# A new order of projection tiles, pooling products inside the attention steps, and an output projection that begins on the pooling groups

## The reference, cut to what matters

```
h = rmsnorm(x);  p, q, k, v = split(h @ w_in)              # 4 x 512 columns
d_g = windowed_mean(p_g, w_g) - p_g                        # 4 pooling groups of 128 columns, w = 2, 4, 8, 16
pool_g = (d_g @ pool_w_g) * pool_scale_g
q, k = rope(q), rope(k)
per head h (4 heads, two score maps each), query block i of 128 rows, keys 0 .. (i+1)*128:
    attn = softmax(q1 k1) - lam * softmax(q2 k2);  o = attn @ v
o = rmsnorm_per_head(o);  x = x + concat(pool_0..3, o_0..3) @ w_o
```

## Time and profile before

| | us |
|---|---|
| three runs | 1964.58, 1962.74, 1958.37 |
| median | 1962.74 |
| the profiled execution's own time | 1960.72 |
| its span, first to last instruction | 1958.6 |
| mean granted TensorE clock | 0.972 |
| first attention step to the end of `wo` | about 50 to 238.6 |

### The profile page before, as it was taken

One profiled execution on the slowest core, in us unless ns is written; L12 is line 12 of the kernel. 1 busy time (PEld: TensorE's weight loads), 2 busy tenths in 40 slices (PEclk: granted clock), 3 DMA queues, 4 the chain that ended last, 5 costly groups with the idle time before them and its releaser, 6 DMA issues.

```text
span 1958.6 us, 23662 instructions
## 1 busy us (share of the span) xinstructions
PE 1836.3 (94%) x8380; PEld 1486.7 (76%) x8380; DVE 1140.8 (58%) x1721; ACT 657.1 (34%) x978; POOL 204.5 (10%) x150
## 2 busy tenths in 40 slices
PE   6996999999999999999999998888898999999986
PEld 4675888888888888888776776667776888888864
DVE  6466668888334655532343777788666655552256
ACT  4333422333223222222333334444444322232242
POOL 3221000000000000000023334444000000000000
PEclk9997999999999999999899999999999999999998
DMA  4676222223322232333222333221241323332221
GB/s 141 71 75 49 86 97 96 96 96 104 102 91 79 97 96 96 100 103 104 80 76 76 105 123 118 69 88 43 93 153 56 108 96 96 96 119 101 90 67 54
DMA packets 55460, 180.62 MB, mean 92 GB/s; under 512 B 6336, under 2 KB 7104, under 8 KB 55392
## 3 DMA queue, kind: packets, MB, share of 16 engines
q1 hardware_dynamic: 43200, 157.07, 24.3%
q10 hardware_dynamic: 12192, 22.67, 7.2%
HBM read 167.65 MB, written 12.06 MB: 92 GB/s over the span
## 4 chain that ended last, share of the span: by engine, by line
PE 77%; DVE 14%; ACT 3%; issue 3%; DMA 2%; ACTq 0%; DVEq 0%; SPq 0%; POOL 0%
PE bank L743 20%; PE bank L744 20%; PE bank L745 20%; PE bank L765 2%; PE bank L767 2%; PE bank L766 2%; PE bank L839 2%; PE bank L840 1%; PE bank L841 1%; DVE score L2206 1%; DMA raw<-in_w_proj 1%; DVE best L2205 1%; PE bank L814 1%; PE bank L1132 1%; DVE chunk L1872 1%
## 5 line engine op out<-in xcount | busy, mean ns | idle before, releaser
L1197 ACT ACTIVATE w_hi<-raw 128x1024 fp32r<-128x1024 f32 (+2 forms) x281 | 304.6, 1087 | 743.7 <-PE bank L745 640.8
L743 PE MATMUL bank<-a_hi,w_hi 128*128 128x512 f32 x1272 | 500.6, 394 | 14.6 <-DVE w_lo L1775 4.9
L745 PE MATMUL bank<-a_hi,w_lo 128*128 128x512 f32 x1272 | 496.6, 390 | 0.0
L744 PE MATMUL bank<-a_lo,w_hi 128*128 128x512 f32 x1272 | 496.6, 390 | 0.0
L1775 DVE TENSOR_TENSOR w_lo<-raw,w_hi 128x1024 fp32r<-128x1024 f32 (+2 forms) x219 | 280.4, 1281 | 253.8 <-ACT w_hi L1197 241.2
L743 PEld LDWEIGHTS bank<-a_hi,w_hi 128*128 128x128 f32 x1272 | 239.7, 188 | 76.8 <-issue 18.9
L745 PEld LDWEIGHTS bank<-a_hi,w_lo 128*128 128x128 f32 x1272 | 239.6, 188 | 50.7
L744 PEld LDWEIGHTS bank<-a_lo,w_hi 128*128 128x128 f32 x1272 | 240.0, 189 | 48.8
L655 POOL TENSOR_TENSOR w_lo<-raw,w_hi 128x1024 fp32r<-128x1024 f32 x54 | 130.0, 2408 | 1071.3 <-ACT w_hi L1197 1071.3
L743 PE MATMUL bank<-h_hi,w_hi 128*128 128x512 f32 x568 | 221.0, 389 | 0.0
L744 PE MATMUL bank<-h_lo,w_hi 128*128 128x512 f32 x568 | 221.0, 389 | 0.0
(11 more groups left out here) (297 smaller groups left out, 2210.6 us busy)
## 6 DMA issues: line engine op xcount, KB each, us to landing
raw<-in_w_up SPq DMA_DIRECT2D x132, 512.0 KB, 3.4
raw<-in_w_down SPq DMA_DIRECT2D x48, 704.0 KB, 4.1
raw<-in_w_proj SPq DMA_DIRECT2D x59, 512.0 KB, 3.5
raw<-in_w_wo SPq DMA_DIRECT2D x8, 512.0 KB, 4.8
raw<-in_w_branch SPq DMA_DIRECT2D x16, 256.0 KB, 2.8
gates_in<-spill ACTq DMA_DIRECT2D x16, 256.0 KB, 3.2
raw<-in_w_out SPq DMA_DIRECT2D x8, 512.0 KB, 3.9
raw<-in_w_ple SPq DMA_DIRECT2D x8, 512.0 KB, 3.4
```

The source lines that it names most:

```text
L743: mm(dst[:, :], wh, hi[:, k, :], start=(first and c == 0), stop=False)
L744: mm(dst[:, :], wh, lo[:, k, :], start=False, stop=False)
L745: step = mm(dst[:, :], wl, hi[:, k, :], start=False, stop=(last and c == n - 1))
L1197: fn(w_hi[:, slot, 0:size], raw[:, slot, 0:size], ACT.Copy).then_inc(unit_high, 1)
```

## The change

The order of the projection tiles becomes q0 k0 v0 q1 k1 p3 v1 q2 k2 p2 v2 q3 k3 p1 v3 p0, the host lays out `w_proj1` in this order, and the steps take 8, 7, 7, 8, 7, 7, 8, 8, 8, 8, 8, 6, 6, 8, 0, 0 chunks, so that the last projection tile ends in step 13. The product of pooling group 3, 2, 1, 0 is done in step 5, 9, 13, 15 respectively; DVE scales it in that step, ACT makes its high part in that step, DVE its low part in the next. The output projection takes the chunks in the order pool 3, 2, 1, 0, heads 0 to 3: tiles 0 to 2 take pool 3 in step 14, pool 2 in step 15, pool 1 in step 16, pool 0 after step 17. Tile 3 takes its four pooling chunks after head 3's sums and ahead of the four `spread` products; then tiles 0 and 1 take the heads' chunks as they come, then tiles 2 and 3. For `mix_hi` of a pooling group to lie over a used q, the q of head h is stored in slot 3-h; `pool_d` shrinks to two buffers and the softmax buffers move up by four tiles.

```diff
-TILES1 = [(kind, h) for h in range(HEADS) for kind in "qkv"] + [("p", g) for g in range(len(WINDOWS))]
+TILES1 = [("q", 0), ("k", 0), ("v", 0), ("q", 1), ("k", 1), ("p", 3), ("v", 1), ("q", 2), ("k", 2), ("p", 2),
+          ("v", 2), ("q", 3), ("k", 3), ("p", 1), ("v", 3), ("p", 0)]
+POOL_ORDER = (3, 2, 1, 0)
+POOL_AT = {5: 3, 9: 2, 13: 1, 15: 0}
+MIX_ORDER = POOL_ORDER + (4, 5, 6, 7)
-FILL1 = spread(LEAD1, len(TILES1), [7] * ATT_STEPS)
+FILL1 = spread(LEAD1, len(TILES1), [8, 7, 7, 8, 7, 7, 8, 8, 8, 8, 8, 6, 6, 8, 0, 0])
-for _g in range(len(WINDOWS)):
-    _aux("pool", _g)
+    if _a in POOL_AT:
+        _aux("pool", POOL_AT[_a])
+        r1.at[0] += len(WINDOWS) * T * 4
# PE
+            def out_part(i, at):
+                first, k = UNIT["wo"][0], MIX_ORDER[at]
+                if at == 0:
+                    wait_bank("wo", i)
+                    pe.wait_ge(unit_split, first + i + 1)
...
+                mm(dst[:, :], wh, mix_hi[:, k, :], start=(at == 0), stop=False)
+                mm(dst[:, :], wh, mix_lo[:, k, :], start=False, stop=False)
+                step = mm(dst[:, :], wl, mix_hi[:, k, :], start=False, stop=(at == DC - 1))
+                if at == DC - 1:
+                    step.then_inc(unit_done, 1)
+            def out_chunk(at, tiles):
+                pe.wait_ge(act_ready, SPLIT["mix1"] + at + 1)
+                for i in tiles:
+                    out_part(i, at)
...
+                if ATT_STEPS - 2 <= a <= ATT_STEPS:            # after fill and aux1
+                    out_chunk(a - ATT_STEPS + 2, range(3))
...
+                if a in POOL_AT:                               # after the turn of a-1
+                    g = POOL_AT[a]
+                    dst = aux_wait("pool", g)
+                    pe.wait_ge(pool_ready, POOL_ORDER.index(g) + 1)
+                    mm(dst[:, :], pool_w[:, g, :], pool_d[:, g % 2, :], start=True, stop=True).then_inc(aux_ready, 1)
...
-                if a == ATT_STEPS:
-                    for g in range(len(WINDOWS)):
-                        dst = aux_wait("pool", g)
-                        pe.wait_ge(pool_ready, g + 1)
-                        mm(dst[:, :], pool_w[:, g, :], pool_d[:, g, :], start=True, stop=True).then_inc(aux_ready, 1)
-            first_three("wo", "mix1", mix_hi, mix_lo, spread_after=(1, 2, 2, 3))
-            for i in range(3, DC):
-                project("wo", i, None, mix_hi, mix_lo)
+            out_chunk(3, range(3))
+            sum_head("head", HEADS - 1)
+            for at in range(HEADS):
+                out_part(3, at)
+            aux_all_free(AUX_ATT)
+            for h in range(HEADS):
+                spread(f"head{h}")
+            for at in range(HEADS, DC):
+                out_chunk(at, range(2))
+            for i in (2, 3):
+                for at in range(HEADS, DC):
+                    out_part(i, at)
+            for i in range(4, DC):
+                project("wo", i, None, mix_hi, mix_lo)
# ACT, end of a step
+                if a in POOL_AT:
+                    g = POOL_AT[a]
+                    high(SPLIT["mix1"] + POOL_ORDER.index(g), mix_hi[:, g, :])
+                if a == ATT_STEPS - 1:
+                    load_root_table()
                 if a == ATT_STEPS:
-                    load_root_table()
-                    highs("mix1", 0, 4, mix_hi)
-            unit_high_part(UNIT["wo"][0] + 3)
+                    unit_high_part(UNIT["wo"][0] + 3)
# DVE
+            def scale_pool(g):
+                c = SPLIT["mix1"] + POOL_ORDER.index(g)
+                dve.wait_ge(aux_ready, AUX["pool", g] + 1)
+                slot_free(c)
+                step(v.tensor_scalar(chunk[:, c % 2, :], aux_bank("pool", g)[:, :], prm("pool_scale", g), None,
+                                     ALU.mult))
+                dve.sem_inc(aux_sem("pool", g), 1)
+                dve.sem_inc(chunk_ready, 1)
...
+                if a - 1 in POOL_AT:                           # after attn of a-1
+                    g = POOL_AT[a - 1]
+                    low(SPLIT["mix1"] + POOL_ORDER.index(g), mix_lo[:, g, :], mix_hi[:, g, :])
...
+                if a in POOL_AT:                               # after rotate, ahead of pool_difference
+                    scale_pool(POOL_AT[a])
...
-            for g in range(4):
-                c = SPLIT["mix1"] + g
-                dve.wait_ge(aux_ready, AUX["pool", g] + 1)
...
-                low(c, mix_lo[:, g, :], mix_hi[:, g, :])
```

More of the change, by code:

```diff
@@ L205 @@
         _aux("bias", _a)
-for _g in range(len(WINDOWS)):
-    _aux("pool", _g)
+    if _a in POOL_AT:
+        _aux("pool", POOL_AT[_a])
+AUX_ATT = len(AUX)
 IDX_STEPS = [(i, h) for i in (3, 2, 1) for h in range(DSA_HEADS)]
@@ L406, in two_blocks @@
         pool_s = r1("pool_s", [P, 2, PAD + T])
-        pool_d = r1("pool_d", [P, 4, T])
+        pool_d = r1("pool_d", [P, 2, T])
         mix_hi = placer(q1_at, q1_at + DC * T * 4)("mix_hi", [P, DC, T], F32R)
@@ L824, in total_x, with first_three @@
                 spread(name)
-            def first_three(stage, split, hi=a_hi, lo=a_lo, spread_after=()):
+            def first_three(stage, split, hi=a_hi, lo=a_lo):
                 first = UNIT[stage][0]
@@ L864, in first_three @@
                         part(3, k - FOURTH_FROM)
[L865 to L870, removed]
             def first_tiles(stage, split, summed=False):
@@ L934, in aux1 @@
                     step.then_inc(aux_ready, 1)
+            def out_part(i, at):
[3 more added lines that the diff above has]
+                    pe.wait_ge(unit_split, first + i + 1)
+                dst, cols = tile_bank("wo", i), slice(k * P, (k + 1) * P)
+                wh, wl = w_hi[:, (first + i) % SLOTS, cols], w_lo[:, (first + i) % SLOTS, cols]
+                mm(dst[:, :], wh, mix_hi[:, k, :], start=(at == 0), stop=False)
[7 more added lines that the diff above has]
+                    out_part(i, at)
             first_three("proj1", "norm1")
@@ L943, in _ @@
                     spread("norm1")
-                    fill("proj1", [(3, 4, 7)])
+                    fill("proj1", [(3, 4, 8)])
                     for t in range(LEAD1):
@@ L953, in _ @@
                         rows = slice(64 * n, 64 * n + 64)
-                        mm(dst[:, 0:end], q1[rows, h, i * P:end], k1[rows, h, 0:end], start=True, stop=False)
+                        mm(dst[:, 0:end], q1[rows, HEADS - 1 - h, i * P:end], k1[rows, h, 0:end], start=True,
+                           stop=False)
                     for dst in scores:
@@ L988, in _ @@
                     sum_head("head", (a - 6) // QB)
-                if a == ATT_STEPS:
-                    for g in range(len(WINDOWS)):
-                        dst = aux_wait("pool", g)
-                        pe.wait_ge(pool_ready, g + 1)
-                        mm(dst[:, :], pool_w[:, g, :], pool_d[:, g, :], start=True, stop=True).then_inc(aux_ready, 1)
-            first_three("wo", "mix1", mix_hi, mix_lo, spread_after=(1, 2, 2, 3))
-            for i in range(3, DC):
+            out_chunk(3, range(3))
[11 more added lines that the diff above has]
+            for i in range(4, DC):
                 project("wo", i, None, mix_hi, mix_lo)
-            hidden("up1", "norm2", AUX["pool", len(WINDOWS) - 1] + 1)
+            hidden("up1", "norm2", AUX_ATT)
             down("down1", 0)
-            hidden("up2", "pre1", AUX["pool", len(WINDOWS) - 1] + 1)
+            hidden("up2", "pre1", AUX_ATT)
             down("down2", 1)
@@ L1944, in rotate @@
                 raw_q = unrot[:, r % 2, :]
-                dst = (q1, k1)[r % 2][:, r // 2, :]
+                dst = k1[:, r // 2, :] if r % 2 else q1[:, HEADS - 1 - r // 2, :]
                 wait(tile_read("proj1", t))
@@ L2016, in _ @@
                             pool_difference(t)
-            for g in range(4):
-                c = SPLIT["mix1"] + g
-                dve.wait_ge(aux_ready, AUX["pool", g] + 1)
[L2020 to L2023, removed]
-                dve.sem_inc(chunk_ready, 1)
-                low(c, mix_lo[:, g, :], mix_hi[:, g, :])
             norm_heads("head", o1, lambda h: prm("attn_norm_g", h), SPLIT["mix1"] + 4, mix_hi, mix_lo)
```

4 lines of the change are left out of this document (2 added, 2 removed).

## The result

The kernel after takes 1948.66 us (median of 6 runs, 1941.56 to 1950.39), against 1962.39 us (6 runs, 1958.37 to 1964.58) for the kernel before: a ratio of 0.9934, 95% interval 0.9916 to 0.9952, so 13.7 us faster. The profiled execution took 1948.33 us, of which 1946.5 are its span; for the kernel before that was 1960.72.

A forecast was written before the change was run, and what follows sets the result against it. PE bounds the kernel, busy 94% of the span. Closing holes and restoring clock: 20.85 - 1.5 - 1.4 - 3.05 - 0.1 = 14.8 us off 1960.72, so 1945.9, plus 2.0 to the median: 1947.9, range 1942.5 to 1957.

The forecast's parts named there:

- The holes and their clock: Last attention steps to head 3's sums: 15.25 us of PE holes plus 5.6 of lower clock, 20.85 to win.
- wo's chunks in steps 14 to 16: Three tiles of a chunk per step where PE waited for DVE; idleness left 0.85, 1.3, 0, plus 0.9 in head chunks: 3.05.
- k one step ahead: k of heads 2 and 3 finished one step before first use: two PE waits of 0.74, 1.5 us lost.
- Values in odd steps: v1, v2, v3 turned in steps 5, 9, 13: waits 2.3, 0.2, 1.0, sum 3.5 against 2.1 before, 1.4 us more.
- The chain of 14.95 us: Bias write issue to ACT's high part begun: 14.95 us; for step 5, write at 78.3, high part at 93.3.
- pooling additions: DVE's pooling differences, moved to steps 4, 8, 12, 14: 2.1 us per addition meeting a GpSimd split, taken as 0.
- The clock: In the tail: no new wait reaches 3.41 us, the shortest after which matmuls ran slow, so 0 lost.
- rival A: Steps 14 to 16 and start of `wo` granted the lower clock: 8 us lost, 1955.9; chance 0.11.
- Tile 4: End of `wo`: tile 4 needs a unit whose slot tile 0 frees; 0.7 less with 0.6 to spare, 0.1 us lost.
- rival E: Early `wo` gain given back at tile 4 by a late unit: 1.6 more lost, 1949.5; inside the forecast's 0.62.
- C: v waits over 3.4 us in steps 5, 9, 13, lower clock after each: 1974.5, or 1966.5 with tail spared; chance 0.06.

The follow-up runs named there:

- late_wo: Kernel after with the early `wo` chunks of tiles 0 to 2 put behind the loop: 1957.2 us, ratio 0.9979 to the kernel before.
- before_warm: Kernel before plus matmuls with unread results where PE waited (24 in step 15, 13 in step 16, 13 before head 3's sums): 1955.57 us, ratio 0.9969.
- rates: Kernel after with 8 chunks in each of steps 0 to 9 and 6 in each of 10 to 13: 1953.74 us.
- bias_even: Kernel after with the bias writes started in even steps (2 to 16) in place of odd ones: 1947.91 us.
- bias_hbm: Kernel after with bias rows written once to HBM in step 1, then copied HBM to HBM in later odd steps: 1938.94 us; run again 1939.5.
- rates_hbm: Kernel after with 8 chunks in steps 0 to 9, 6 in 10 to 13, and bias rows copied HBM to HBM: 1940.67 us.

## Why the prediction was right

The forecast was 1947.9 us and 14.8 us won in the profile; measured are 1948.66, and 13.2 by the end of `wo`. The mechanism held: holes closed by `wo` chunks, and the clock with them. Two costs were missing from the sum: a wait of 2.14 us in step 4, and a fall of the clock in step 12. The steps one by one:

- *The holes and their clock.* Right in kind and size. late_wo shows that work in the holes closes them, and before_warm that the clock is a price of its own. before_warm gave back 3.4 of the 5.6 us, with 1.7 of them paid again in its second fall. The two profiles bear out the sum: waits of 0.4 us and more between 50 us and the end of `wo` come to 19.3 before and 9.9 after, 9.3 less, so that 3.9 of the 13.2 is left for the clock, which is 5.6 won in the tail less the 1.7 lost in step 12 (an estimate, as smaller waits are left out).
- *wo's chunks in steps 14 to 16.* Forecast 0.85, 1.3 and 0 of idleness, 0.9 more in the head chunks; measured 0.72, 1.26, 0.51 and 0 (195 to 226 us is busy throughout). 2.5 for 3.05.
- *k one step ahead.* Forecast 2 x 0.74 = 1.5; measured 0.90 and 1.45, 2.35 together. What they hold above 0.74 is a GpSimd split beside DVE's last operation on k, which took 0.85 and 1.40 us in place of 0.69 (split of 2.66 from 144.80):

```profile
146.61 1.40 DVE L1991 TENSOR_TENSOR k<-k,silu 128x512 f32<-128x512 f32 x1
```

- *Values in odd steps.* Forecast three waits, 3.5 in all, the longest in step 5; measured 0.91 and 0.46 in steps 5 and 9, none in step 13, so 1.4 us. The chain of 14.95 us was as predicted (write issued 78.32, high part begun 93.32, 15.0), but PE wanted the bank at 94.75 and not at 93.1: the wait of 2.14 in step 4 had delayed it. One wait ate the other.
- *The wait before step 4's turn*, 2.14 us. Not in the sum. The prediction bounded DVE beside a GpSimd split only for pooling additions (2.1 each, taken as 0); the split hit the chain to `attn` instead. With the 0.9 on k, splits beside DVE cost 3.0 us in this kernel, the largest thing the forecast left out. One addition did meet a split in step 12, without cost to PE:

```profile
156.00 2.76 DVE L2003 TENSOR_TENSOR pool_s<-pool_s 128x512 f32<-128x512 f32 x1
```

- *The clock.* "Nothing of the new waits reaches 3.41 us", hence no loss: right in the tail, wrong as a bound. After the wait of 1.45 us (148.06) the clock was granted at 0.50 for some 3.4 us, from about 149.5 to 152.9, which cost about 1.7 us. By what happened in the tail rival A is out: short waits in a row left it at 1.00 there. The passage of the Trainium skill that the prediction weighed (page "TensorE: Matmul & The Clock Gate", section "HAM oscillation — how this bites in real kernels") tells of half rate behind waits of some 3 to 5 us between short bursts. late_wo agrees with it, with waits of 3.0 and 3.5; the tail of the kernel after, with waits of 1.26 us and less, is not that case, and it stayed at full rate (PE busy 8.17 of 10 at 1.00). The prediction left the length of those waits out when it drew rival A from the section.
- *Tile 4.* Its low part was ready at 202.62 (201.39 + 1.23 in the DVE timeline) and it began at 202.79, without a wait, 0.2 to spare: rival E is out, narrowly.

Summed: 20.85 - 2.35 + 0.7 (v: 1.4 for 2.1) - 2.5 - 2.1 - 1.7 = 12.9, against 13.2 measured at the end of `wo`. The forecast had 14.8. The errors cancelled in part: too pessimistic on the values by 2.1 and on the tail by 0.6, too kind by 0.9 on k, 2.1 on the turn and 1.7 on the clock. That the median came within 0.8 us is partly luck. For the profiled execution the forecast was 1945.9, and it took 1948.33, 2.4 more; the forecast then added 2.0 for the distance from profile to median, which was 0.3 this time. The later attention moves by up to 4 us from kernel to kernel as well. C, slower than before, never had its condition: no v wait exceeded 0.91 us. Its price was real, though: rates and bias_even show single waits of 4.01 and 4.36 us on the same copy, after small moves of the tiles or writes. A forecast could rule them out only by following loads, writes and bank uses step by step.

## What to carry to other kernels

Where PE waits for a chain on another engine in a row of steps, look for later products whose inputs are complete early and put them in those holes: here three tiles of a chunk in each of three steps brought 10.7 us of 13.2 in the profile, and the new order by itself nothing. Before tuning rates, look at what makes the loads late: here a write that took 13.7 us held up the loads beside it, and the cheaper copy was worth about 9 us on top of the 13.7 that the change had won, while two other sets of rates won nothing. And when an operation shows several times its usual duration, look at what GpSimd does at that moment.

## What the runs showed of the hardware

- Writing one row of 2.5 KB of SBUF 128 times to HBM (320 KB) took 13.7 us from issue to landing, and loads of 512 KB on another queue took 9.0 instead of 3.4 meanwhile; the same 320 KB from HBM to HBM took 4.0. The Trainium skill, page "SBUF — State Buffer", section "Door 1: The DMA port swizzle", has the reach in SBUF ports set a transfer's rate, 27.2 GB/s for one port, and its section "The DMA setup-cost knee" adds some 2 us of fixed cost. A row lies in one partition, so 327,680 bytes would take 12.0 + 2 = 14.0 us by the page, an estimate that agrees with the 13.7 measured. That others' loads are slowed as well is what the trace adds.
- DVE's operations beside a GpSimd split: 2.29 us for 128 single elements (0.16 otherwise), 2.56 for a scaling of 128x512 (0.49 otherwise), 2.12 and 2.76 for additions of 128x512 (0.69 otherwise). Each began while a split ran and ended within 0.6 us of the split's end, the small one as the large one: they waited rather than ran slower. Additions with both operands in SBUF and scalings were hit; the operation that reads PSUM (0.69 at 103.44, split from 103.37) was not. The Trainium skill, page "SBUF — State Buffer", section "Who interferes with whom", says this: DVE and GpSimd share a pair of ports as an exclusive lock, which operations with two inputs in SBUF want and the scaling forms can want. The trace agrees, with 2.29 us for 128 elements as the plainest case.
- The clock after equal waits: in bias_hbm the wait of 1.45 us before step 12's scores left it at 1.00, in the second profile of the very same kernel it fell, and in both profiles of the kernel after as well. The wait of 2.14 at 85.35 left it at 1.00, but behind the waits of 2.14 and 2.15 at 89.6 in rates_hbm and rates it was 0.50 from 90 to 93 us. In before_warm it fell behind a wait of 0.90. Second profile of bias_hbm, window of the five us behind that wait:

```profile
144.00:149.00 5.00, 5.00 (x19) 3.86 (x20) 2.45 (x8) 0.91 (x4) 0.00 (x0) 0.66 0.14 36
```

So the length of one wait did not decide it, and a forecast has to hold a fall possible behind waits of 0.9 to 1.5 us; what decides it no run here shows. Between these two executions of one kernel the end of `wo` lies 1.2 us apart (219.84 and 221.04).
